# FFN output: five groups per pass, with the second and fourth weight sums added by DMA in the first sum's buffer

## The reference, cut to what matters

```python
def swiglu_ffn(x, w_in, w_out):
    gate, up = jnp.split(x @ w_in, 2, axis=-1)
    return (jax.nn.silu(gate) * up) @ w_out      # w_out: (5504, 2048), x: 256 tokens

x = x + 0.5 * swiglu_ffn(rmsnorm(x, ffn1_norm[l]), ffn1_w_in[l], ffn1_w_out[l])
...                                              # projections, attention, w_out
x = x + 0.5 * swiglu_ffn(rmsnorm(x, ffn2_norm[l]), ffn2_w_in[l], ffn2_w_out[l])
```

## Time and profile before

| what | value |
|---|---|
| median of 3 runs | 1753.33 us (1752.81 to 1753.72) |
| the profiled execution's own time | 1753.02 us |
| its span, first to last instruction | 1751.2 us |
| PE busy | 1742.3 us (99%) |
| DVE busy | 1473.4 us (84%) |
| ACT busy | 1106.5 us (63%) |
| POOL busy | 94.9 us (5%) |
| DMA traffic | 405.03 MB |

### The profile page before, as it was taken

The page is one execution under the profiler, slowest core; times in us unless marked ns, Lnnn a source line. Parts: engine busy times, 40 slices in busy tenths (PEclk is TensorE's granted clock), DMA queues, the critical chain, the costliest instruction groups (busy, mean ns, idle before and its releaser), DMA issues.

```text
span 1751.2 us, 21435 instructions
## 1 busy us (share of the span) xinstructions
PE 1742.3 (99%) x7976; PEld 1451.8 (83%) x7976; DVE 1473.4 (84%) x1778; ACT 1106.5 (63%) x1461; POOL 94.9 (5%) x111
## 2 busy tenths in 40 slices
PE   9999999999999999999999999999999999999999
PEld 7888888888888888888888888888888888988887
DVE  7999889998999998575655655898999898899998
ACT  7676666766666666454545554667676676666665
POOL 0000100000000001100000000010000000000000
PEclk9999999999999999999999999999999999999999
DMA  9899899997555556555454558689999898764762
GB/s 378 255 294 275 260 264 265 265 277 236 210 212 201 197 215 210 186 186 178 160 185 161 176 175 298 207 264 263 267 277 278 272 282 239 251 210 159 257 218 90
DMA packets 168327, 405.03 MB, mean 231 GB/s; under 512 B 9016, under 2 KB 18000, under 8 KB 162848
## 3 DMA queue, kind: packets, MB, share of 16 engines
q1 hardware_dynamic: 154208, 342.03, 54.3%
q0 software_dynamic: 12896, 59.67, 17.2%
q10 hardware_dynamic: 1120, 1.97, 0.3%
HBM read 351.57 MB, written 5.79 MB: 204 GB/s over the span
## 4 chain that ended last, share of the span: by engine, by line
PE 95%; DVE 3%; DMA 1%; ACT 0%; issue 0%; SPq 0%; POOL 0%; DVEq 0%; ACTq 0%
PE bank L699 8%; PE bank L700 8%; PE bank L701 8%; PE bank L726 8%; PE bank L728 7%; PE bank L727 7%; PE bank L660 7%; PE bank L662 7%; PE bank L661 7%; PE bank L806 5%; PE bank L808 5%; PE bank L807 5%; PE bank L833 3%; PE bank L834 3%; PE bank L832 3%; DVE wlo L1363 1%
## 5 line engine op out<-in xcount | busy, mean ns | idle before, releaser
L1363 DVE TENSOR_TENSOR wlo<-raw,whi 128x1024 fp32r<-128x1024 f32 (+1 forms) x466 | 559.8, 1208 | 179.4 <-ACT whi L1002 173.6
L1002 ACT ACTIVATE whi<-raw 128x1024 fp32r<-128x1024 f32 (+1 forms) x466 | 486.3, 1047 | 304.1 <-PE bank L662 189.2
L726 PE MATMUL bank<-whi,xs 128*128 128x512 f32 (+1 forms) x528 | 205.6, 389 | 3.0 <-DVE wlo L1363 2.3
L728 PE MATMUL bank<-whi,xs 128*128 128x512 f32 (+1 forms) x528 | 203.1, 385 | 0.0
L727 PE MATMUL bank<-wlo,xs 128*128 128x512 f32 (+1 forms) x528 | 202.9, 384 | 0.0
L806 PE MATMUL bank<-whi,aw_hi 128*128 128x512 f32 x420 | 164.0, 390 | 0.0
L808 PE MATMUL bank<-whi,aw_lo 128*128 128x512 f32 x420 | 163.5, 389 | 0.0
L807 PE MATMUL bank<-wlo,aw_hi 128*128 128x512 f32 x420 | 163.4, 389 | 0.0
L660 PE MATMUL bank<-whi,xs 128*128 128x512 f32 x384 | 155.1, 404 | 0.4 <-DVE wlo L1363 0.4
L662 PE MATMUL bank<-whi,xs 128*128 128x512 f32 x384 | 150.0, 391 | 0.0
L661 PE MATMUL bank<-wlo,xs 128*128 128x512 f32 x384 | 149.5, 389 | 0.0
(11 more groups left out here) (257 smaller groups left out, 3541.6 us busy)
## 6 DMA issues: line engine op xcount, KB each, us to landing
raw<-ffn_w_in SPq DMA_DIRECT2D x86, 1024.0 KB, 6.8
raw<-ffn_w_out SPq DMA_DIRECT2D x84, 1024.0 KB, 6.4
raw<-w_in SPq DMA_DIRECT2D x48, 1024.0 KB, 5.0
raw<-ffn_w_in SPq DMA_DIRECT2D x75, 512.0 KB, 7.4
tsum<-raw POOLq DMA_DIRECT2D x35, 1024.0 KB, 7.9
minis<-ffn_w_in SPq DMA_DIRECT2D x72, 256.0 KB, 7.5
last_plain<-ffn_w_in SPq DMA_DIRECT2D x36, 512.0 KB, 9.3
raw<-w_out SPq DMA_DIRECT2D x16, 1024.0 KB, 5.0
```

Source lines behind the costliest of these rows:

```text
L726: mm(banks[b][:, 0:w], xs[:, k + i, 0, tok], hi, start=starts[b] and k + i == 0, stop=False, skip_group_check=True)
L728: last = mm(banks[b][:, 0:w], xs[:, k + i, 1, tok], hi, start=False, stop=k + i == last_k, skip_group_check=True)
L1002: A(hi_of(h)[:, 0:n_el], src, ACT.Copy).then_inc(weights_hi, 1)
L1363: V.tensor_tensor(lo_of(h)[:, 0:n_el], src, hi_of(h)[:, 0:n_el].bitcast(f32), ALU.subtract).then_inc(weights_lo, 1)
```

## The change

- Five groups instead of four in both passes; 23 plain items remain in each pass. Pass 1 takes its groups in the order 4, 1, 2, 3, 0, because the store for the activation sums keeps four groups (`KEPT`); the sums of group 0 are made a second time in pass 1.
- The products are reordered: T1, B11, (T4 of the group before), plain, T3, B22, plain, T2, B21, plain. Groups follow each other with nothing between; only the first has plain items in front (6 in pass 0, 5 in pass 1). The last T4 of a pass comes behind the plain item that follows B21, and two (pass 0) or three (pass 1) plain items are left behind it.
- The signs are turned so that all weight sums are additions. T1's sum lies in one half of `tsum` (`out_half_sum`, halves taken in turn by groups). T2's sum is made by a DMA that adds B22 to it when T1's `wlo` has been written, and T4's sum by a DMA that adds B21 when T2's `wlo` has been written. DVE's sums for T2 and T4 are gone. Each DMA is 512 KB and is issued by POOL; its source is one column half of a raw piece, two stretches of 2 KB per partition.
- A group's first raw piece is free when T3 is split, its second when T4 is split (before: when T4's sum was made, and when B22 was split). B11's activation split covers only one token block.
- The steps of `join` come later relative to the last items.

```diff
-OUT_GROUPS = (4, 4)
+GROUP_IDS = ((0, 1, 2, 3, 4), (4, 1, 2, 3, 0))
+OUT_GROUPS = tuple(len(ids) for ids in GROUP_IDS)
-LEADS = ((6, 2, 2, 2), (5, 2, 2, 2))
+LEADS, BETWEEN = (6, 5), (0, 0)
+KEPT = 4
+SUMS_AT = [(0, g) for g in range(OUT_GROUPS[0])] + [(1, KEPT)]
...
+    items = [("plain", next(plain)) for _ in range(LEADS[c])]
     for g in range(OUT_GROUPS[c]):
+        items += [("form", g, "T1"), ("form", g, "B11")] + ([("form", g - 1, "T4")] if g else [])
+        for forms in (("T3", "B22"), ("T2", "B21"), ()):
+            items += [("plain", next(plain))] + [("form", g, f) for f in forms]
+        items += [("plain", next(plain)) for _ in range(BETWEEN[c] if g + 1 < OUT_GROUPS[c] else 0)]
+    return items + [("form", OUT_GROUPS[c] - 1, "T4")] + [("plain", k) for k in plain]
...
+JOIN_FROM = [OUT_ITEMS[c].index(("form", OUT_GROUPS[c] - 1, "T2")) + 4 for c in range(PASSES)]
+JOIN_STEPS = [{JOIN_FROM[0]: (0,), JOIN_FROM[0] + 1: (1, 2)},
+              {JOIN_FROM[1]: (0,), JOIN_FROM[1] + 1: (1, 2), JOIN_FROM[1] + 2: (3,)}]
...
-                        if q < 2 * OUT_GROUPS[c] and q % 2 == 0:
-                            return out_sums, 4 * group(u, c, q // 2) + 4
-                        item = ("form", q // 2, "B22") if q < 2 * OUT_GROUPS[c] else ("plain", min(2 * q + 1, FT - 1))
+                        item = ("form", q // 2, ("T3", "T4")[q % 2]) if q < 2 * OUT_GROUPS[c] else ("plain", min(2 * q + 1, FT - 1))
...
+            def out_adds(u):
+                for c in range(PASSES):
+                    for g in range(OUT_GROUPS[c]):
+                        G, n1 = group(u, c, g), out_piece(u, c, 2 * g + 1)
+                        pool.wait_ge(weights_lo, out_half(u, c, ("form", g, "T1")) + 1)
+                        pool.wait_ge(raw_full[raw_slot(n1)], RAW_FULL[n1])
+                        pool.dma_start(out_half_sum(G), quarter(n1, 1), accum_op=ALU.add).then_inc(out_t2, 16)
+                        pool.wait_ge(weights_lo, out_half(u, c, ("form", g, "T2")) + 1)
+                        pool.dma_start(out_half_sum(G), quarter(n1, 0), accum_op=ALU.add).then_inc(out_t4, 16)
...
-                            if f in ("T1", "T3", "T2", "T4"):
-                                act_e.wait_ge(out_sums, 4 * G + 1 + ("T1", "T3", "T2", "T4").index(f))
+                            if f in ("T1", "T3"):
+                                act_e.wait_ge(out_sums, 2 * G + (1 if f == "T1" else 2))
+                            if f == "T2":
+                                act_e.wait_ge(out_t2, 16 * (G + 1))
+                            if f == "T4":
+                                act_e.wait_ge(out_t4, 16 * (G + 1))
...
-                        if i == T4_ENDS[c] - 1:
+                        if i == JOIN_FROM[c] - 1:
                             copy_p1(u, c)
...
-                if f == "T2":
-                    dve.wait_ge(out_sums, 4 * G + 2)
-                    dve.wait_ge(weights_lo, out_half(u, c, ("form", g, "B11")) + 1)
-                    V.tensor_tensor(B11, B12, B11, ALU.add).then_inc(out_sums, 1)
-                if f == "T4":
-                    dve.wait_ge(out_sums, 4 * G + 3)
-                    V.tensor_tensor(pair(tsum[:, 2 * W:4 * W]), B21, B11, ALU.subtract).then_inc(out_sums, 1)
...
-                        if t4 < i <= t4 + 6:
-                            join(u, c, i - t4 - 1)
-                        if c and i < 6 - (OUT_LEN[0] - 1 - T4_ENDS[0]):
-                            join(u, 0, OUT_LEN[0] - 1 - T4_ENDS[0] + i)
-                for step in range(OUT_LEN[1] - 1 - T4_ENDS[1], 6):
+                        for step in JOIN_STEPS[c].get(i, ()):
+                            join(u, c, step)
+                        if c and i < 3:
+                            join(u, 0, 3 + i)
+                for step in (4, 5):
                     join(u, 1, step)
```

More of the change, by code:

```diff
@@ L169, in raw_slot @@
     if n >= IN_P[1]:
-        return (0, 2, 1, 3, 4, 5, 0, 1)[n - IN_P[1]]
+        oldest = (FIRST_OUT_SLOT - sum(ACT_PLAIN) - (IN_P[1] - QKV_P)) % QKV_RAW_SLOTS
+        return (*((oldest - i) % QKV_RAW_SLOTS for i in range(3)), 3, 4, 5, 0, 1)[n - IN_P[1]]
     return (FIRST_OUT_SLOT - sum(ACT_PLAIN) - (n - QKV_P)) % QKV_RAW_SLOTS if n >= QKV_P else n % RAW_SLOTS
@@ L1675, in ffn_out @@
                             n0, n1 = out_piece(u, c, 2 * g), out_piece(u, c, 2 * g + 1)
-                            src = {"T1": pair(tsum[:, 0:2 * W]), "B11": quarter(n0, 0), "T3": quarter(n0, 1), "T2": quarter(n0, 0),
-                                   "B21": quarter(n1, 0), "B22": quarter(n1, 1), "T4": pair(tsum[:, 2 * W:4 * W])}[f]
+                            own = out_half_sum(group(u, c, g))
+                            src = {"T1": own, "B11": quarter(n0, 0), "T3": quarter(n0, 1), "T2": own,
+                                   "B21": quarter(n1, 0), "B22": quarter(n1, 1), "T4": own}[f]
                             dve.wait_ge(weights_hi, h + 1)
```

112 lines of the change are left out of this document (53 added, 59 removed).

## The result

The changed kernel takes **1771.49 us** (median of 4 runs, 1768.37 to 1773.01), the kernel before 1753.53 (1752.81 to 1754.05): a ratio of 1.0100, 95% interval 1.0085 to 1.0115, so 18 us slower. The prediction was 1759, with a range of 1749 to 1768: the sign was right, the size was not, and the time lies outside the range. The profiled execution took 1773.01 us, its span 1771.2. Two of the five executions of one experiment (e15) ran at a far lower clock and took 2177 and 3037 us; they are left out.

A forecast was written before the change was run, and what follows sets the result against it. The prediction took PE, busy 99%, as the bound, with DVE tied in pass 0. Terms -5.4 + 2.0 + 3.3 + 1.4 + 0.4 + 4.1 = +5.8 on 1753.0 gave 1758.8, predicted as 1759 us; 8-in-10 range 1749 to 1768.

The forecast's parts named there:

- PE's work: FFN outputs: one more group in each of four passes removes 24 matmuls at 0.227 us, -5.4 us.
- DVE in pass 0: Pass 0 of each FFN output: DVE stays tied with PE, 1.0 us of PE waiting per pass, +2.0 us.
- How long an add takes: Each 512 KB DMA add: 16 packets per engine at 0.30 us plus 1.8, 6.5 us with no load beside it.
- The last T4 of a pass: End of each pass: add may take 6.0 us, takes 6.5; PE waits there and for ACT's work behind, +3.3 us.
- the prediction's own signs of being wrong: Adds landing in under 6 us, last T4's lead over 2.9 us, or waits in the middle of pass 1.
- The lead that is lost: Three places after a late T4 empties the ring: start of pass 1 +1.4, next projection +0.4, very end +4.1 us.
- the start of pass 1: T4's low part to B11's: DVE about 22.4 us for 21.8 of PE, 0.6 to 0.9 per FFN, +1.4 us.
- The turn to the next projection: Behind the first FFN: joins now end close to PE's last item, +0.4 us (0 to 1.5).
- The very end: After the last T4 of the last pass: a plain item's cover is gone and the lead is nothing; PE waits +4.1 us.
- S + 2.7: Very end: time in us when the last k-tile is due in PE's first bank, if T4 starts at S.
- Where nothing is expected: ACT, DMA, SP's loads and POOL: no cost; DMA needs 15.6 to 19.2 us for 17.7, a near thing.
- The third rival: Adds and loads collide, delaying T4 in 16 groups and the last T4s: 1775 us, half of it 1767; chance 0.2.

The follow-up runs named there:

- e15: Changed kernel with the 40 sums made by GpSimd as instructions on 128x1024 instead of by DMA; 1824.09 us.
- e8: Changed kernel without adds, bank-by-bank end over two k-tiles instead of three, one more plain item behind the last T4; 1751.44 us.
- e1: Changed kernel with its 40 adds left out, T2 and T4 split from T1's sum, ScalarE waiting for no add; 1754.56 us.
- e6: Changed kernel with four groups in both passes instead of five, two plain items between groups, adds kept; 1760.19 us.
- e9: Changed kernel with all 40 adds issued into an unread half of the sum buffer, ScalarE waiting for none; 1762.53 us.
- e16: Changed kernel with SyncE loading over a group's second piece once T4's add has landed and B21 is split; 1775.19 us.
- e4: Changed kernel with the bank-by-bank end over the last two k-tiles instead of three; 1768.83 us.
- e12: Changed kernel with the sums of T2 and T4 made by VectorE again in the second pass of both FFNs, five groups; 1769.78 us.
- e2: Changed kernel with each add cut to the first of two rows of a partition, 256 KB; 1759.58 us.
- e5: Changed kernel with the second FFN's output product reading the first FFN's output weights; 1765.43 us.
- e3: Changed kernel with each group's second piece loaded in two transfers, so add sources lie in 4 KB stretches; 1780.58 us.

## Why the prediction was wrong

**PE's work** was right in what it removes: 24 matmuls, and PE was the bound. In e8's stretches 2.5 of the 5.4 us arrive, 1.6 in the first FFN's output and 0.9 in the second's. Of the other 2.9, 2.7 are VectorE's lateness in pass 0, the next term.

**DVE in pass 0** held, and was a little undersized. I took 1.0 us per pass 0. In the first FFN the trace has four waits of 0.13, 0.21, 0.18 and 0.17 at plain items, 1.6 us by the starts; the first three recur in e1, at 0.12 to 0.20, and in e8. The two passes of e8 have 2.7 us for my 2.0.

**How long an add takes** was wrong in its price. I chose 0.30 us for a 2 KB packet, from a window that I took for one in which such a DMA ran alone, against 0.18 beside a load, and got 6.5 us. That window has 196 packets of a load in it too, 30.3%. An add that is really alone, in 524.9 to 528.5 us:

```profile
q0 software_dynamic: 270, 0.52, 79.9%
...
tsum<-raw POOLq DMA_DIRECT2D x1, 512.0 KB, 4.8
```

0.799 x 16 x 3.6 / 256 = 0.18 us a packet; 16 x 0.18 + 1.8 would have been 4.7, and 4.8 to 5.1 us is what adds take alone. A window's share over its packets is a packet's price only while packets are there all the time. The Trainium skill, page "DMA: Bandwidth & Descriptors", section "Anatomy of one DMA — SWDGE (gpsimd) path", has a fit for a DMA of this path, with nothing said of adding, that would give 3.2 us as an estimate; the traces don't agree with it, by 1.6 us.

**The last T4 of a pass**, +3.3, was thus wrong in size: in the first FFN none is late, in the second one is, by 0.55 us. The mechanism was right: the prediction allows 6.0 us from T2's low part to T4's split, at the very last T4 (T2's low part ends at 1743.50) it was 1748.66 - 1743.50 = 5.16, and the difference, 0.84 us, is the lead that was left. Two of the prediction's own signs of being wrong came true: adds alone land in under 6 us, and waits stand in the middle of pass 1. **The lead that is lost** was right at the start of pass 1: waits of 0.37 and 0.61 us at T1, 0.61 and 0.85 by the starts, for 0.6 to 0.9. The turn to the next projection cost nothing; its waits of 0.4 us are those of before. The terms of the first FFN, -2.7 + 1.0 + 1.65 + 0.7 + 0.4, give +1.1, and it measured +1.2, which is luck in part: pass 0 cost 1.6, the turn nothing, and the stalls at T4 and a plain item, 1.5 in all, sat in the middle of pass 1 and not at the last T4s.

**The very end** was right in place and near in size, 3.63 us for 4.1, with two errors that offset each other. T4's lead was not nothing but 0.84 us. And PE doesn't go on to S + 2.7, where the last tile's `wlo` is due: the program makes it wait for the low part of the last activation tile before the first matmul of the bank-by-bank end, at S + 1.36. VectorE has that 5.9 us behind T4's low part, not 6.8: 5.9 - 0.84 - 1.36 = 3.7. What follows the wait was left out: the half clock. From T4 to the end the changed kernel should take 15.72 - 2.72 (one plain item) = 13.0; it took 19.40. That is 6.4 us, so 2.8 beyond the wait, 2.6 of it the clock. Of the wait, 1.6 us hang on the add and 2.0 on the order: without adds (e1) T4's lead is 2.9 us and PE still waits 2.0, where I had put 1.2. e6, with one more k-tile behind T4 and nearly no waits in the middle, has the 3.6 us too: there as well ScalarE waits 3.7 us for the last add, and T4's lead is 0.9, and the k-tile more is no cover, since VectorE's splits and the two updates of x that come with it take as long as PE's 2.7 us.

**"Where nothing is expected"** holds the step that failed: the collision of loads and adds was put at nothing in the sum. I compared 8 to 11 us between a load's issue and its use with "6.4 us", one median over both FFNs of a kernel without adds. Split by FFN the same trace has 5.2 and 6.5, and with adds beside them loads have medians of 6.3, 7.5, 7.7 and 8.3 us in the four windows and up to 14.42. I had even worked out the engines' time, 15.6 to 19.2 us for 17.7, called it near, and left it out of the sum. It costs 7.9 us by e9, 1.5 of them the clock at its end. The other 9.0 are adds late beside loads (up to 10.9 us in the second FFN) and the part of the end that hangs on them, with its share of the half clock.

**The third rival** had the mechanism, adds and loads in each other's way, with a price of 1775 and half of it 1767; 1771.5 lies between. It was wrong in where: it put the waits evenly at 16 groups and four last T4s, behind adds alone, and gave loads no part. With 0.2 for it, and a range that ended at 1768, I had priced it and not reached to it.

## What to carry to other kernels

A transfer that was moved onto the DMA engines was paid here by all transfers beside it too. Price it as its own latency, as the added latency of every load in the same stretch, and per stage, since one median hides the stage without slack. With 23.1 us per group a mean DMA share of 0.74 to 0.77 was nearly harmless, and with 17.7 one of 0.79 to 0.86 cost most of the 18 us. The mean share gives little warning, then; I would look at the time that each load has from issue to use, though no run here isolates it. Issuing loads earlier didn't help (e16). First bound a change by leaving its costs out (e8): here 2.3 us was all that this order had to give, since VectorE's lateness in pass 0 took another 2.7. And measure stalls by the starts of the matmuls: a list of waits missed 0.24 us of each.

## What the runs showed of the hardware that was not expected

- A stall can cost more than itself. After 3.63 us without matmuls the granted clock is at 1.2 GHz for the next matmuls (0.54 and 0.77 in two windows of 5 us), worth 2.6 us here; after 0.9 us (e4) it stays at 1.00. After 2.0 us both occurred, with the same order of matmuls: it stayed in e1 and e12 and fell in e2 and e9. In the middle of a pass it stayed after 2.7 us (the changed kernel) and 3.4 (e4) and fell after 2.0 (e5) and 3.5 (e16), so the length of the wait alone doesn't decide it. The windows of 1745 to 1750 us of e1 and of e9:

```profile
1745.00:1750.00 5.00, 5.00 (x24) 4.14 (x23) 3.72 (x6) 0.00 (x0) 0.00 (x0) 1.00 0.17 66
```

```profile
1745.00:1750.00 5.00, 3.04 (x9) 2.14 (x8) 5.00 (x9) 0.29 (x1) 0.00 (x0) 0.75 0.00 0
```

- Loads of the same size and form from another tensor of the same kernel took 8.3 instead of 6.1 us in the same stretch (the changed kernel and e5).
- Loads in rows of 2 KB instead of 4 KB, and twice as many of them, cost more than adds from stretches of 4 KB instead of 2 KB gave back (e3, +9 us).
- Two engines that read SBUF at once can hold each other up: with GpSimd adding, VectorE's sum of two 128x1024 operands took 2.10 us instead of 1.22, and GpSimd's own 3.2 and 7.0 us in the mean at its two places. The Trainium skill, page "SBUF — State Buffer", section "Who interferes with whom", says that an instruction of VectorE with two inputs in SBUF contends with a GpSimd instruction that reads SBUF; e15 agrees.
